# Last attention units: both score pairs ahead of the division, and the modulation pieces in units 0 to 2

## What is computed

```python
s = jnp.einsum('nbqhgd,nbkhd->nbhgqk', qb, kw) * (dh ** -0.5) + bias
s = jnp.where(mask, s, NEG)
m = s.max(axis=-1)                 # layer 0: also the sink
p = jnp.exp(s - m[..., None])
l = p.sum(axis=-1)                 # layer 0: plus exp(sink - m)
o = jnp.einsum('nbhgqk,nbkhd->nbqhgd', p, vw) / l
```

## Time and profile before

| | us |
|---|---|
| median of 3 runs (2821.97 to 2825.81) | 2823.31 |
| the profiled execution's own time | 2823.84 |
| its span | 2821.8 |
| PE busy in the span | 2692.6 (95%) |
| DVE busy | 1948.1 (69%) |
| ACT busy | 1012.4 (36%) |
| POOL busy | 271.9 (10%) |

### The profile page before, as it was taken

How to read it: one execution, slowest core, us unless ns; L and a number is a source line. 1 busy time by engine, 2 the same in 40 slices (tenths; PEclk the granted TensorE clock), 3 DMA queues, 4 the chain that set the end, 5 groups by cost and what they waited for, 6 DMA issues and landing times. The chain is left out here.

```text
span 2821.8 us, 35472 instructions
## 1 busy us (share of the span) xinstructions
PE 2692.6 (95%) x12770; PEld 2120.5 (75%) x12770; DVE 1948.1 (69%) x3279; ACT 1012.4 (36%) x1789; POOL 271.9 (10%) x422
## 2 busy tenths in 40 slices
PE   6999699999999999999998989999999999999798
PEld 5666377788888888766675768888888878879767
DVE  6787747877778777667767597777777784331653
ACT  5554424333333332444444253333333341101232
POOL 2110000000000001101100000000000049920000
PEclk9999899999999999999998899999999999979899
DMA  5223321111111111223221111111111131121212
GB/s 225 98 98 101 138 90 53 49 52 50 55 51 52 56 48 49 97 68 98 91 82 75 34 38 57 51 56 52 48 56 52 49 113 38 45 46 32 82 38 75
DMA packets 172826, 193.08 MB, mean 68 GB/s; under 512 B 7952, under 2 KB 138224, under 8 KB 172432
## 3 DMA queue, kind: packets, MB, share of 16 engines
q1 hardware_dynamic: 160160, 147.45, 16.1%
q0 software_dynamic: 12560, 44.20, 5.1%
HBM read 177.86 MB, written 12.58 MB: 67 GB/s over the span
## 5 line engine op out<-in xcount | busy, mean ns | idle before, releaser
L2085 DVE SCALAR_TENSOR_TENSOR xT<-psum,mod,xT 128x1024 f32<-128x1024 f32 x352 | 446.6, 1280 | 143.0 <-PE psum L1255 143.0
L1255 PE MATMUL psum<-hT_high,w_low 128*128 128x512 f32 x1344 | 360.0, 390 | 4.1 <-DVE xT L2085 4.1
L1255 PEld LDWEIGHTS psum<-hT_high,w_low 128*128 128x128 f32 x1344 | 251.8, 188 | 58.6 <-DVE xT L2085 6.6
L1613 ACT ACTIVATE w_high<-wpair 128x512 fp32r<-128x512 f32 x294 | 184.6, 632 | 227.2 <-DMA wpair<-in_ffn_w_in_dram 129.4
L1036 PE MATMUL psum<-hT_high,w_low 128*128 128x512 f32 x944 | 260.2, 395 | 2.1 <-DVE arena L2481 2.1
L1036 PEld LDWEIGHTS psum<-hT_high,w_low 128*128 128x128 f32 x944 | 179.4, 191 | 40.5 <-DVE arena L2481 2.3
L1255 PE MATMUL psum<-h_low,w_low 128*128 128x512 f32 x672 | 207.6, 390 | 2.3 <-DVE h_low L2080 2.3
L1083 PE MATMUL psum<-hT_high,w_low 128*128 128x512 f32 x480 | 203.7, 424 | 1.9 <-DVE h_low_mix L2369 1.2
L1223 PE MATMUL psum<-hT_high,w_high 128*128 128x512 f32 x504 | 196.8, 391 | 3.5 <-DVE w_low L2045 3.5
L1732 ACT ACTIVATE arena<-arena 128x384 f32<-128x384 f32 (+3 forms) x320 | 157.7, 494 | 116.3 <-DVE arena L2266 116.3
L1224 PE MATMUL psum<-h_low,w_high 128*128 128x512 f32 x504 | 196.6, 390 | 0.0
(11 more groups left out here) (340 smaller groups left out, 5261.1 us busy)
## 6 DMA issues: line engine op xcount, KB each, us to landing
wpair<-in_ffn_w_in_dram SPq DMA_DIRECT2D x176, 256.0 KB, 2.9
wpair<-in_ffn_w_out_dram SPq DMA_DIRECT2D x88, 256.0 KB, 2.8
wpair<-in_ada_tiles_dram POOLq DMA_DIRECT2D x20, 1024.0 KB, 5.4
wpair<-in_ada_tiles_dram POOLq DMA_DIRECT2D x32, 512.0 KB, 3.6
wpair<-in_w_in_dram SPq DMA_DIRECT2D x24, 512.0 KB, 3.8
wpair<-in_b_tiles_dram SPq DMA_DIRECT2D x18, 512.0 KB, 3.3
arena<-in_ada_tiles_dram SPq DMA_DIRECT2D x8, 1024.0 KB, 16.4
out_dram<-xT SPq DMA_DIRECT2D x16, 512.0 KB, 3.0
```

The lines of the kernel that those rows point to most:

```text
L1255: mm = nc.tensor.matmul(dst[:, HALF * t:HALF * t + HALF], w, src[:, t, :], start=n == 0, stop=n == 2)
L1613: nc.scalar.activation(part_high[name], part_raw[name], ACT.Copy).then_inc(part_high_ready, 1)
L2085: nc.vector.scalar_tensor_tensor(xT[:, m, :], acc[m % 2] if src is None else src, mod[:, l, 40 + m:41 + m], xT[:, m, :], ALU.mult, ALU.add ...
```

## The change

Two things are edited. In the last unit of each call (`alone`: unit 3 and unit 9) PE issues scores(t, 0), outputs(t - 2), scores(t, 1), turn(t - 1), and DVE issues biased(t, 0), biased(t, 1), normalised(t - 1), outputs(t - 2). And the 20 pieces are laid on units 0 to 2 as 7, 7 and 6, at every n but 1; POOL's transfers are grouped the same way, and unit 3 has none.

```diff
-                for k in range(5):
-                    m = 5 * u + k
+                for m in range(7 * u, min(7 * u + 7, 20)):
...
-                    ahead = t // 8 + 1 < last
+                    ahead, alone = t // 8 + 1 < last, t >= 8 * last - 8
                     if t < 8 * last:
                         scores(t, 0)
                     if ahead:
                         project(t // 8 + 1, 2 * (t % 8))
+                    if alone:
+                        outputs(t - 2)
                     if t < 8 * last:
                         scores(t, 1)
-                    if t - 2 >= 8 * first:
+                    if not alone and t - 2 >= 8 * first:
                         outputs(t - 2)
...
+                    alone = t >= 8 * last - 8
                     if t < 8 * last:
                         biased(t, 0)
-                    if 8 * first <= t - 1 < 8 * last:
+                    if not alone and t - 1 >= 8 * first:
                         normalised(t - 1)
                     if t < 8 * last:
                         biased(t, 1)
+                    if alone and t - 1 < 8 * last:
+                        normalised(t - 1)
                     if t - 2 >= 8 * first:
                         outputs(t - 2)
...
-                    if t < 32 and n in (0, 2, 4, 6, 7):
-                        piece(5 * u + (0, 2, 4, 6, 7).index(n))
+                    if t < 23 and n != 1:
+                        piece(7 * u + (0, 2, 3, 4, 5, 6, 7).index(n))
```

## The result

The change makes the kernel slower. Its median is 2849.24 us over four runs (2846.68 to 2855.44), against 2822.64 for the kernel before beside it; the ratio is 1.0095 with a 95% interval of 1.0077 to 1.0114. The profiled execution is the longest of the four, 2855.44 us, with a span of 2853.4; the other three took 2846.68 to 2850.39. So the trace explains 31.6 us of span, of which the median shows 26.6.

What follows compares the result with a forecast made beforehand. PE, busy 95% of the span, was taken to bound the kernel, so only stretches where it waits count. Terms 0.2 + 1.0 + 7.2 + 8.8 + 5 = 22.2 us gave 2845.5 us, range 2830 to 2860.

Steps and rivals of the forecast that it cites:

- Units 0 to 2: Added pieces delay DVE some 0.35 us at tile 4, mostly hidden from PE: +0.2 us, bounds 0 and 12.
- The pieces' own gain: Unit 3 without pieces, old order kept: 56 us for 73.05, or 17 us less.
- Unit 3's loop: New order makes a serial loop through PE, DVE and ACT: 8.87 us a wide tile against 6.02, +1.0 us in all.
- Rival 4: Unit 3's loop is shorter, some 8.0 us a tile at full clock: 2824.5 us, no change; chance 0.06.
- rival 2: New order costs nothing, division not on the path, and the pieces' gain stays: 2806 us, faster; chance 0.07.
- Unit 9's loop: New order makes a serial loop in unit 9: 4.85 us a tile against 3.65 at full clock, about +7.2 us.
- the signs that the prediction named: Trace marks expected in the changed kernel, among them unit 9's tiles 4.7 to 6 us apart, its length 41 to 47.
- The clock in unit 3: PE's idle time in the new loop lowers the clock: half of 17.7 us taken, +8.8 us.
- the bound of 17.7: Unit 3 wholly at the low clock: 2.2 us more a tile, eight tiles, 17.7 us.
- The clock in unit 9: Low clock costs 1.8 us a tile, 14.5 in all; a third taken as spare products fill PE: +5 us.
- Part 2: The prediction's section on the new order in unit 3, a serial loop summed step by step: 74.0 us against 73.05.

Runs made afterwards that it cites:

- e1: The change's move of the pieces alone, old order kept in both last units, against the kernel before: 2808.16 us, ratio .9943.
- e6: The change plus unneeded matmuls on PE ahead of each turn, 12 a tile in unit 3, 6 in unit 9: 2835.83 us, 1.0037 to the kernel before.
- e4: The change's new order in both last units, pieces laid back where the kernel before had them: 2852.93 us, ratio 1.0101 to that kernel.
- e5: The change with the new order in unit 9 only, unit 3 in the old order, pieces moved: 2824.13 us, ratio 1.0001 to the kernel before.
- e2: The change with PE's half of the order only (outputs between the pairs), DVE's division in its old place: 2828.49 us, 1.0011 to the kernel before.
- e3: The change with DVE's half of the order only (division behind the second pair), PE's order old: 2836.61 us, 1.0044 to the kernel before.
- e7: e2 with ACT copying the turned tile ahead of the next exponentials in the last units: 2821.42 us, ratio .9990 to the kernel before.

## Why the prediction was right, and where its terms were off

The sign, the mechanism and the range held; the predicted 22.2 us stand against 26.6 in the median and 31.6 in the profiled execution.

- **Units 0 to 2**: +0.2 forecast, -0.3 measured. The row of 0.35 us of delay came out: in unit 2 DVE takes up tile 4 at 244.25 us, 9.37 behind tile 3's first head, where it was 9.00. It does not reach PE, which had no idle time from 206 to 279.
- **The pieces' own gain**: 17 us forecast, unit 3 of 56; e1 measured 16.6 and 56.45, and the four kernels with that unit 3 make it 15.0 to 17.5.
- **Unit 3's loop**: 8.87 us a wide tile forecast, 8.82 measured; the waits inside it, 0.7 and 3.5 us forecast, are 0.69 and 3.38. The unit at full clock: 74.0 forecast, 74.35 in e6 (at 0.98). Rival 4, a loop of 8.0 us, and rival 2, no cost, both fell here.
- **Unit 9's loop**: 4.85 forecast, 4.73 measured where the clock was full. Low tiles of 7.12 us and a unit of 50.20 lie outside the signs that the prediction named (tiles of 4.7 to 6, a unit of 41 to 47 us); e4 and e5, with 47.3, are just at the edge.
- **The clock in unit 3** was the first term that was mis-sized: 8.8 taken, 85.74 - 74.35 = 11.4 measured. I priced a turn at the low level by the 2.07 us of the earlier trace rows, a turn in which the clock had come back midway. It takes 2.82, so a low tile pays 1.3 for its turn where I had 0.5, and the bound of 17.7 was too low. Taking half of the bound was a choice without a row behind it; with the right price, half would have been 12. A mean of 0.78 between levels of 0.5 and 1 means that 44% of the unit ran low, so that the half was near the truth was luck.
- **The clock in unit 9** was the second: 5 taken, a third of 14.5. With a loop of 41 us at full clock the profiled execution paid some 9, and e4 and e5 some 6. Here too the prices were too small: a tile at the low level takes 7.12 us against 4.73, 2.4 more and not 1.8. Taking a third had no row behind it either: by the same reckoning 48% of the unit ran low in the change and 28% in e4 and e5. My reason for so little, that the spare products fill PE, is not borne out by the change, which has them behind the turn and 0.76. In e6 six more matmuls a tile ahead of the turn, beside those, go with 0.92; whether their place or their number does it is not separated.
- **Behind unit 9** 2.9 us more passed in the profiled execution; the same order in e4 shows 0.6, so I don't put it down to the change. It and the 3 us that unit 9 is longer than in e4 and e5 are about what the profiled execution has above the median. That the other three runs lack just these was not seen, since they have no trace.

One step was missing and did no harm. Rival 2 named the division alone as what could cost something, and Part 2 counted the copy as a wait of 0.7 us. e2 shows that the outputs' new place, which seemed the harmless half, costs 20 us by itself, with the loop through ACT's order in both units. In the change the longer loop covers it. At full clock the halves add 1.95 and 1.48 us to a wide tile of 6.02, and both together 2.80, less than their sum of 3.43: the longer loop sets the pace. The whole times do not show this. The halves' 20.3 and 28.4 us over e1 make 48.7; the change lies 41 to 45 us over e1, by which median of the kernel before one takes, and in the lengths of the two units the halves make 17.8 + 26.9 = 44.7 us and the change 45.6, since the clock falls differently in each.

It stays open how the clock's spells fall. e3 left unit 3 at 1.00, where its turns waited 1.41 us in each tile, and unit 9 at 0.61, where no wait of a tile was longer than 0.54 in the low stretch shown; the change left them at 0.78 and 0.76. e4 and e5 have the change's order in unit 9 and 0.86. From the rows of before I could bound this and not size it.

## What to carry to other kernels

When a step is moved in one engine's order, write down every cycle that closes over the engines' orders, with each engine's own queue in it (here the copy behind the next tile's exponentials), and take the longest; the shares of busy time show none of them. Opening one such loop can close another: the copy moved ahead of the exponentials in e7 made one of 7.40 us. Idle time inside such a loop on TensorE can be paid twice, as the wait and as the lower clock behind it: in the change's unit 3 some 18 us (56.45 to 74.35) for the one and 11.4 for the other; in e3's unit 3 the clock stayed at 1.00. Side work that looks free should be moved to where another engine sets the pace before the order around it is touched: the pieces alone gave 0.5 to 0.6%, and leaving unit 3 was worth about 1 us in a loop that had idle time enough to hide them (e4).

## What the runs showed of the hardware

- Twelve transposing matmuls of 128 columns took 1.53 us at the upper level (2.4 GHz) and 2.82 at the lower (1.2 GHz); the spare products 1.03 and 1.91. From start to start, with the overlap of the rows left out, the turns took 1.46 and 2.75 us and the spare products 0.96 and 1.84, a ratio of 1.88 and 1.92, less than two.
- A stretch of 10.60 us with a granted clock of 0.74 and one of 8.82 us with 0.98 held the same work, two wide tiles of the same kernel, one after the other. So the cost of a loop has to be read from several of its turns.
- Filling PE's wait in unit 3 with 12 matmuls a tile that nobody needs made the unit 11.4 us shorter.
- In e3's unit 9 the granted clock was 0.50 for 29 us in which PE's waits were 0.49 to 0.54 us, two in a tile of 6.64; in e3's unit 3 it was 1.00 with waits of 1.41 us. No run here explains the difference.
